# Where the causal mask of a sparse-attention loop is added: identity products on TensorE, or one VectorE add per step

## The reference, cut to what matters

```python
m_s = (key_pos <= tq[None, None, :, None, None]).reshape(B, G, 1, T, k_top * SEL_LEN)
s_s = jnp.einsum('btghd,bgtnkd->bghtnk', qb, k_sel) * scale
p_s = masked_softmax(s_s.reshape(B, G, HPG, T, k_top * SEL_LEN), m_s)
...
s_w = jnp.einsum('btghd,bsgd->bghts', qb, kwb) * scale
p_w = masked_softmax(s_w, m_w)
...
o = gb[..., 0:1] * o_c + gb[..., 1:2] * o_s + gb[..., 2:3] * o_w
```

## Time and profile before

| what | value |
|---|---|
| median of three runs | 2953.64 us (2951.76 to 2955.32) |
| the profiled execution | 2953.68 us |
| its span (first to last instruction) | 2951.9 us |
| PE busy in the span | 2858.2 us, 97% |
| DVE busy in the span | 1376.6 us, 47% |
| ACT busy in the span | 983.6 us, 33% |

### The profile page before, as it was taken

The page is one execution under the profiler, slowest core; times in us unless marked ns, Lnnn a source line. Parts: engine busy times, 40 slices in busy tenths (PEclk is TensorE's granted clock), DMA queues, the critical chain, the costliest instruction groups (busy, mean ns, idle before and its releaser), DMA issues. The chain is left out here.

```text
span 2951.9 us, 37772 instructions
## 1 busy us (share of the span) xinstructions
PE 2858.2 (97%) x14556; PEld 2353.7 (80%) x14556; DVE 1376.6 (47%) x1827; ACT 983.6 (33%) x1571; POOL 474.3 (16%) x363
## 2 busy tenths in 40 slices
PE   7999999998999999999999997999999999999998
PEld 5888888887876688888877875888888788888887
DVE  4464543335557754333445555443334465443333
ACT  4322432225145543222322323332223433332222
POOL 0021122100111212221011221022210012022210
PEclk9999999999999999999999998999999999999999
DMA  4323233333510023333232221233332332233331
GB/s 146 93 85 94 70 107 95 96 100 107 142 44 1 1 65 107 99 90 101 85 100 79 85 67 55 86 93 97 93 98 90 103 90 86 79 93 99 98 93 59
DMA packets 459669, 256.07 MB, mean 87 GB/s; under 512 B 9632, under 2 KB 447632, under 8 KB 459424
## 3 DMA queue, kind: packets, MB, share of 16 engines
q1 hardware_dynamic: 455488, 246.50, 28.5%
q10 hardware_dynamic: 3456, 5.77, 0.7%
q0 software_dynamic: 608, 2.16, 0.2%
HBM read 248.11 MB, written 2.10 MB: 85 GB/s over the span
## 5 line engine op out<-in xcount | busy, mean ns | idle before, releaser
L1443 DVE TENSOR_TENSOR w_lo<-w_raw,w_hi 128x1024 fp32r<-128x1024 f32 x461 | 626.0, 1359 | 943.9 <-ACT w_hi L1058 943.4
L478 PE MATMUL acc<-a_hi,w_hi 128*128 128x512 f32 x2264 | 890.1, 393 | 8.3 <-DVE y_lo L1899 5.1
L480 PE MATMUL acc<-a_hi,w_lo 128*128 128x512 f32 x2264 | 880.0, 389 | 0.0
L479 PE MATMUL acc<-a_lo,w_hi 128*128 128x512 f32 x2072 | 807.0, 389 | 0.0
L1058 ACT ACTIVATE w_hi<-w_raw 128x1024 fp32r<-128x1024 f32 x461 | 483.5, 1050 | 521.6 <-PE acc L480 462.5
L478 PEld LDWEIGHTS acc<-a_hi,w_hi 128*128 128x128 f32 x2264 | 426.2, 188 | 101.1 <-issue 12.8
L480 PEld LDWEIGHTS acc<-a_hi,w_lo 128*128 128x128 f32 x2264 | 425.6, 188 | 88.4
L479 PEld LDWEIGHTS acc<-a_lo,w_hi 128*128 128x128 f32 x2072 | 389.7, 188 | 79.8 <-issue 1.4
L480 PE MATMUL acc<-hid_hi,w_lo 128*128 128x512 f32 (+1 forms) x704 | 264.5, 376 | 0.0
L479 PE MATMUL acc<-hid_lo,w_hi 128*128 128x512 f32 (+1 forms) x704 | 264.5, 376 | 0.0
L478 PE MATMUL acc<-hid_hi,w_hi 128*128 128x512 f32 (+1 forms) x704 | 264.5, 376 | 0.0
(11 more groups left out here) (302 smaller groups left out, 3484.7 us busy)
## 6 DMA issues: line engine op xcount, KB each, us to landing
w_raw<-ffn_w_gate SPq DMA_DIRECT2D x88, 512.0 KB, 3.8
w_raw<-ffn_w_up SPq DMA_DIRECT2D x88, 512.0 KB, 3.8
w_raw<-gm_w_in SPq DMA_DIRECT2D x64, 512.0 KB, 4.0
w_raw<-ffn_w_down SPq DMA_DIRECT2D x64, 512.0 KB, 3.8
w_raw<-ret_w_in SPq DMA_DIRECT2D x48, 512.0 KB, 3.8
w_raw<-gm_w_out SPq DMA_DIRECT2D x32, 512.0 KB, 3.7
w_raw<-ffn_w_down SPq DMA_DIRECT2D x32, 384.0 KB, 3.3
w_raw<-nsa_w_in SPq DMA_DIRECT2D x21, 512.0 KB, 3.9
```

Source lines behind the costliest of these rows:

```text
L478: pe.matmul(o_bank, lhs_hi, rhs_hi, start=start, stop=False)
L479: pe.matmul(o_bank, lhs_hi, rhs_lo, start=False, stop=False)
L480: return pe.matmul(o_bank, lhs_lo, rhs_hi, start=False, stop=stop)
L1443: dve.tensor_tensor(w_lo[:, slot, :, :], w_raw[:, slot, :, :], w_hi[:, slot, :, :].bitcast(f32), ALU.subtract).then_inc(lo_done, 1)
```

## The change

The identity products M are taken out of PE's list. DVE adds the mask instead, in place in PSUM, one operation per step over both heads: 2 x 128 elements per partition in kinds 0 and 1, and 2 x 256 in kind 2. It does so between the end of S and the row maximum, and the maximum waits for it on a semaphore of DVE itself (`link`). S now signals once for each head (`s_even`, `s_odd`), since the last product of each half of the array may end on its own. The second part of kind 2 begins its own accumulation instead of relying on a product that follows. ACT no longer makes the two tables `causal_r` and `ident_r` (lines 1287 and 1288).

```diff
-                pe.wait_ge(mask_r, 2)
...
                         for c, col in PARTS[kind]:
                             for x in range(2):
-                                pe.matmul(bank[:, x, col:col + (c + 1) * P], nq[side_of(x), hp, c * P:(c + 1) * P],
-                                          kd[side_of(x), br, hp // 2, 0:(c + 1) * P], start=c > 0, stop=False)
-                        for x in range(2):
-                            c, wide_mask = PARTS[kind][0][0], len(PARTS[kind])
-                            last = pe.matmul(bank[:, x, c * P:(c + wide_mask) * P], ident_r[:, :], causal_r[:, 0:wide_mask, :], start=False, stop=True)
-                        last.then_inc(s_mm, 1)
+                                last = pe.matmul(bank[:, x, col:col + (c + 1) * P], nq[side_of(x), hp, c * P:(c + 1) * P],
+                                                 kd[side_of(x), br, hp // 2, 0:(c + 1) * P], start=True, stop=True)
+                                if c == PARTS[kind][-1][0]:
+                                    last.then_inc([s_even, s_odd][x], 1)
...
-                        if u == 4:
-                            act.wait_ge(n_tab_in, 16 * 7)
-                            act.activation(causal_r[:, :, :], causal[:, :].unsqueeze(1).broadcast_to([P, 2, P]), ACT.Copy).then_inc(mask_r, 1)
-                            act.activation(ident_r[:, :], ident[:, :], ACT.Copy).then_inc(mask_r, 1)
...
-                        dve.wait_ge(s_mm, s + 1)
+                        dve.wait_ge(s_even, s + 1)
+                        dve.wait_ge(s_odd, s + 1)
                         wait(dve, exp_done, exps_through(s - 4))
+                        c, wide_mask = PARTS[kind][0][0], len(PARTS[kind])
+                        blocks = bank[:, :, c * P:(c + wide_mask) * P].rearrange("p x (m k) -> p x m k", k=P)
+                        link(dve.tensor_tensor(blocks, blocks, causal[:, :].unsqueeze(1).unsqueeze(1).broadcast_to([P, 2, wide_mask, P]), ALU.add))
                         for i, (c, col) in enumerate(PARTS[kind]):
                             last = dve.tensor_reduce(nm[:, s % 4, 2 * i:2 * i + 2], bank[:, :, col:col + (c + 1) * P], AX.X, ALU.max, negate=True)
                         last.then_inc(max_done, 1)
```

More of the change, by code:

```diff
@@ L276, in build @@
         kr = place("kr", [P, G_NSA, N_CMP], f32, B + 63 * KB + 512)
-        causal_r = place("causal_r", [P, 2, P], f32r, B + 73 * KB)
-        ident_r = place("ident_r", [P, P], f32r, B + 64 * KB)
         causal = place("causal", [P, P], f32, B + 64 * KB + 512)
@@ L320, in build @@
             o_sum r_mean_mm r_mu_ready ro_cen ro_sq ro_csum r_var_mm r_var_rd r_root r_sd_ready ry_done rg_done y_hi_done y_lo_done
-            n_tab_in n_zero rot_even rot_odd rope_t n_rope kd_dup kc_done nv_tr nv_done sig_done gt_done mask_r
+            n_tab_in n_zero rot_even rot_odd rope_t n_rope kd_dup kc_done nv_tr nv_done sig_done gt_done
             stg_ready cmp_mm h1_done kcmp_mm kcmp_x kcmp_rot kcmp_done vcmp_mm vblk_done
             sc_even sc_odd sm_done pexp pc_done pc_tr pc_t pvc_mm ocmp_done dve_step
-            s_mm max_done exp_done t_mm pt_done pv_mm rs_inv spread_mm spread_done o_rd o_add o_hi_done o_lo_done
+            s_even s_odd max_done exp_done t_mm pt_done pv_mm rs_inv spread_mm spread_done o_rd o_add o_hi_done o_lo_done
             y_tr y_sb stored""".split()
@@ L336, in build @@
          o_sum, r_mean_mm, r_mu_ready, ro_cen, ro_sq, ro_csum, r_var_mm, r_var_rd, r_root, r_sd_ready, ry_done, rg_done, y_hi_done, y_lo_done,
-         n_tab_in, n_zero, rot_even, rot_odd, rope_t, n_rope, kd_dup, kc_done, nv_tr, nv_done, sig_done, gt_done, mask_r,
+         n_tab_in, n_zero, rot_even, rot_odd, rope_t, n_rope, kd_dup, kc_done, nv_tr, nv_done, sig_done, gt_done,
          stg_ready, cmp_mm, h1_done, kcmp_mm, kcmp_x, kcmp_rot, kcmp_done, vcmp_mm, vblk_done,
          sc_even, sc_odd, sm_done, pexp, pc_done, pc_tr, pc_t, pvc_mm, ocmp_done, dve_step,
-         s_mm, max_done, exp_done, t_mm, pt_done, pv_mm, rs_inv, spread_mm, spread_done, o_rd, o_add, o_hi_done, o_lo_done,
+         s_even, s_odd, max_done, exp_done, t_mm, pt_done, pv_mm, rs_inv, spread_mm, spread_done, o_rd, o_add, o_hi_done, o_lo_done,
          y_tr, y_sb, stored) = [s[n] for n in names]
```

## The result

The changed kernel takes 2963.17 us in the median of six runs (2962.18 to 2964.84), the kernel before 2951.49 us in the median of its six (2949.02 to 2955.32). The ratio is 1.0038, with a 95% interval of 1.0026 to 1.0051: slower by 11 us, between 8 and 15. The profiled execution took 2963.58 us with a span of 2961.6 us, against 2953.68 and 2951.9. So 9.9 of the 11 us can be looked for in the two traces.

What follows compares the result with a forecast made beforehand. The loop was taken as bound by a ring through DVE, ACT and PE, with PE near its limit. 2953.7 plus 10.5 us for the longer ring plus 6.4 for clock falls gave 2970.6, said as 2970; range 2959 to 2979.

Steps and rivals of the forecast that it cites:

- the ring: Loop group as a chain through DVE, ACT and PE: grows 0.63 us from 9.89, 10.1 us over 16 groups.
- rival (a): The clock stays at its full level in the loop, so only the 10.5 us are added: 2964 us; chance 0.27.
- The adds: DVE's mask adds ahead of the maxima: 0.42 us for 256 elements and 0.69 for 512.
- The add of kind 0: Its 0.46 us lies in DVE's idle time, because T waits for exp of kind 2.
- The terms within the ring: Per group, 0.45 us for the add of kind 1 and 0.18 us for that of kind 2.
- the wait of 0.47 us: DVE's wait for M of kind 2, between the scaling's end and the maximum of kind 2, in each group.
- The clock: PE's gap ahead of T of kind 2 grows to 1.95 us; half of 16 gaps lower the clock: 6.4 us.
- rival (c): Adds of kinds 1 and 2 cost so little that the group gets shorter: 2946 us at no cost; chance 0.09.
- the PE bound: Variant of rival (c): PE sets the loop's time, so 14.4 us go, 2939 us; faster had chance 0.04.

Runs made afterwards that it cites:

- e3: Changed kernel with the DVE add for kind 1 alone, identity products on PE for kinds 0 and 2; 2951.56 us, ratio 1.0001 to the kernel before.
- e4: Changed kernel with the DVE add for kind 2 alone, identity products on PE for kinds 0 and 1; 2959.98 us, ratio 1.0024 to the kernel before.
- e5: Changed kernel with the add of kind 2 done twice; 2982.97 us, ratio 1.0107 to the kernel before.
- e1: Changed kernel without the add, so no mask at all; 2945.75 us, ratio 0.9978 to the kernel before.
- e6: Changed kernel with the reciprocal and `SS` moved ahead of the copy of kind 2; 2958.23 us, ratio 1.0023 to the kernel before.
- e7: Kernel before the change with the reciprocal and `SS` moved ahead of the copy of kind 2; 2960.95 us, ratio 1.0033.
- e2: Kernel before the change, identity products kept, with the DVE add also in front of each maximum and S signalling per head; 2966.54 us, ratio 1.0045.
- e12: Changed kernel: S of kinds 2 and 0 and maximum of kind 2 earlier, kind 0 mask on PE, reciprocal and `SS` before copy of kind 2; 2941.06 us.

## Why the prediction was right, and where it was not

The forecast was 2970 us, in the range from 2959 to 2979. Measured were 2963.17 us. The direction and the mechanism of the ring were right. What came true is rival (a), the ring without the clock, at 2964 us; the 2965 to 2976 that the forecast had as its own range was missed. That 2964 lies within 1 us of the measurement is in part luck. The forecast started from 2953.7 us, the median of three runs, and the kernel before has 2951.49 in six; the increase of rival (a) was 10.5 us and the measured one is 11.7.

- **The adds.** 0.42 and 0.69 us were taken from the nearest rows, and the same are measured. Writing back to PSUM costs nothing extra: the in-place add of 512 elements takes 0.69 us, like the scaling, which writes to SBUF. The 65 ns more that the prediction estimated from the Trainium skill, page "Perfetto Trace Analysis", section "Optimizing Scalar/DVE Operations", do not show in these rows.
- **The ring.** 0.63 us a group was forecast and 0.64 measured, 9.5 us against 9.84 over the 15 groups between the first and the last copy of kind 2. The add of kind 0 is hidden as said: DVE has its 0.96 us of idle time ahead of the copy.
- **The terms within the ring.** The sum charged 0.45 to kind 1 and 0.18 to kind 2. e3 and e4 show 0.04 and 0.40 by themselves, the second with 0.21 of waiting for S of kind 2. The split depends on which is moved first, as the wait of 0.47 us can be used once; the sum does not.
- **The clock, the step that failed.** "PE is idle for 1.95 us in each group" was too long by 0.3 us, and of the falls behind "about half of the 16 gaps" none came in the middle of the loop: 6.4 us too much. The other five executions cannot have had eight falls either. Eight stretches of 3.4 us at half the clock would take 0.005 off the mean granted clock; their means are 0.989 to 0.991, that of the profiled execution is 0.989, and those of e5 are 0.985 to 0.987. For the length of the gap three things were missed. T of kind 0 still waits for the copy of kind 2 (0.19 us of idle time before 946.59), so the removal of M of kind 1 brings PE nothing. From the start of the four transposes of kind 1 to PV it is 0.70 us now (950.12 to 950.82), against 0.53 before (943.72 to 944.25). Of this the transposes themselves take 0.06: where they follow the scores directly and nothing else holds PV, it is 0.59 us in e1, and so it is in e4 and e6. The other 0.11 is the third thing: PV of kind 0 writes the bank that the scaling reads and waits for it, and the scaling now ends only at 950.67.
- **What decides a fall stays open.** That the shorter gap is the reason for the missing falls is not shown. In the two profiled executions the same three gaps of 1.74 us outside the loop changed places: the two that end at 314.12 and 1904.93 us lowered nothing before, and in the changed kernel the clock fell behind them; behind the one that ends at 2565.59 it fell before and not after. So the length of the gap alone does not decide, and a share of falls taken from five gaps was a weak ground for 16 others. That falls happen inside the loop is shown by e5: with gaps of 2.23 to 2.38 us it has seven, at about 1 us each. The Trainium skill, page "TensorE: Matmul & The Clock Gate", section "Why this matters for your kernels", warns only of gaps above about 3 us; the fall behind the 2.38 us before 984.60 disagrees with it.
- **The cheaper add of rival (c) and the PE bound.** Both are excluded, by the add's rows and by e1: even with no mask at all the loop gains 0.36 us a group, not 0.90.

What stays open is the rest between the 9.9 us of the profiled executions and the 11.7 of the medians; it is within the interval of the ratio. Why the clock fell at 871.5 us in the first group, and not in the same place before, was not tried; e7 has a fall at 870.6 us too, where the longest gap of PE in the 8 us ahead is 1.24 us, and e1 has none, with the gap of 1.61.

## What to carry to other kernels

Before work is moved off the engine with the highest busy share, follow one turn of the loop through all engines. Where the turn closes over other engines, taking work from the busy one gives only the wait at its end (0.36 of 0.90 us here), and what is put on the ring is paid in full. A wait can hide one addition, not two, so terms must be summed along the ring and not one by one. And the same edit can change its sign with the order of the work: 0.64 us a group lost while the ring was closed, 0.17 gained once the scores of two kinds and one maximum had been moved one place forward.

## What the runs showed of the hardware that was not expected

- A VectorE add in place in PSUM took 0.69 us for 512 elements, as long as a multiplication from PSUM to SBUF (the scaling) or from SBUF to SBUF (`SS`), and 0.42 for 256.
- In the changed kernel 14 gaps of PE of 1.65 and 1.74 us left the granted clock at 1.00. In e5 14 gaps of 2.23 to 2.38 us brought it to 0.50 seven times, at about 1 us a fall. Single falls came behind gaps of 1.59 us (e2) and 1.61 us (the changed kernel), and the same gap of 1.74 us was followed by a fall in one execution and by none in the other.
- Four transposes took 0.59 us up to the next product behind products with 64 rows, and 0.53 behind products with 128.
- A VectorE operation with two SBUF inputs that started behind a GpSimd subtraction was 2.1 and 2.6 times as long (e7, e12). When it started first, it kept its 0.69 us, and the subtraction took 1.75 us instead of 1.27 (e6).
